# Two matmuls in place of three per 128 rows of weights in the feed-forward layers of 256 tokens

## The reference, cut to what matters

```python
def conv_ffn(h, w_up, conv_w, conv_b, w_down):
    u = h @ w_up                       # 1024 -> 2 * 2816 features
    ...
    for j in range(CONV_W):            # CONV_W = 3 taps over the tokens
        acc = acc + up[:, j:j + L] * conv_w[j]
    a, g = jnp.split(acc, 2, axis=-1)
    return (jax.nn.silu(g) * a) @ w_down
```

## Time and profile before

| | us |
|---|---|
| median of 3 runs | 1633.01 |
| lowest and highest run | 1632.73 and 1633.6 |
| span of the profiled execution | 1629.6 |
| TensorE busy in it | 1587.4 |
| VectorE busy | 1047.1 |
| ScalarE busy | 809.9 |

### The profile page before, as it was taken

The page is one execution under the profiler, slowest core; times in us unless marked ns, Lnnn a source line. Parts: engine busy times, 40 slices in busy tenths (PEclk is TensorE's granted clock), DMA queues, the critical chain, the costliest instruction groups (busy, mean ns, idle before and its releaser), DMA issues.

```text
span 1629.6 us, 27020 instructions
## 1 busy us (share of the span) xinstructions
PE 1587.4 (97%) x10876; PEld 1372.2 (84%) x10876; DVE 1047.1 (64%) x1952; ACT 809.9 (50%) x1537; POOL 236.8 (15%) x282
## 2 busy tenths in 40 slices
PE   7999999999999999999999999999999999999998
PEld 4788778877777888887899988878999898799986
DVE  3734856465345434787787767766777667767765
ACT  2414963432233323567455554655555566555553
POOL 0202320011010100012011101142111013311110
PEclk9999999999999999999999999999999999999999
DMA  9765022354564323021455453334555543345552
GB/s 365 290 247 208 24 77 103 155 207 155 207 232 181 103 97 136 27 79 53 164 185 212 169 201 124 131 105 155 182 181 182 197 140 123 133 146 187 182 194 78
DMA packets 39852, 257.29 MB, mean 158 GB/s; under 512 B 5552, under 2 KB 6832, under 8 KB 11056
## 3 DMA queue, kind: packets, MB, share of 16 engines
...
## 4 chain that ended last, share of the span: by engine, by line
PE 85%; DVE 9%; ACT 4%; issue 1%; DMA 1%; ACTq 0%; POOL 0%; DVEq 0%; SPq 0%
PE ps L486 25%; PE ps L488 25%; PE ps L487 25%; PE ps L502 3%; PE ps L634 1%; PE ps L656 1%; PE ps L643 1%; DVE ps L2101 1%; PE ps L1109 1%; DVE wl L1848 1%; PE ps L528 1%; DMA raw<-in_ada 1%; PE ps L615 1%; ACT wh L1374 1%; ACT arena L1445 1%
## 5 line engine op out<-in xcount | busy, mean ns | idle before, releaser
L1842 DVE TENSOR_TENSOR wl<-raw,wh 128x1024 fp32r<-128x1024 f32 (+3 forms) x318 | 371.1, 1208 | 346.1 <-ACT wh L1374 345.5
L1374 ACT CAST wh<-raw 128x1024 fp32r<-128x1024 f32 (+2 forms) x328 | 322.7, 1033 | 489.0 <-PE ps L488 399.2
L486 PE MATMUL ps<-xh,wh 128*128 128x256 f32 (+1 forms) x1582 | 493.6, 312 | 3.7 <-DVE wl L1848 3.2
L488 PE MATMUL ps<-xh,wl 128*128 128x256 f32 (+1 forms) x1582 | 488.6, 309 | 0.0
L487 PE MATMUL ps<-xl,wh 128*128 128x256 f32 (+1 forms) x1582 | 488.5, 309 | 0.0
L486 PEld LDWEIGHTS ps<-xh,wh 128*128 128x128 f32 x1582 | 301.8, 191 | 28.9 <-issue 9.3
L487 PEld LDWEIGHTS ps<-xl,wh 128*128 128x128 f32 x1582 | 302.0, 191 | 15.1 <-issue 0.7
L488 PEld LDWEIGHTS ps<-xh,wl 128*128 128x128 f32 x1582 | 301.9, 191 | 15.2
L486 PE MATMUL ps<-wh,xh 128*128 128x512 f32 (+3 forms) x812 | 298.6, 368 | 2.0 <-issue 0.8
L488 PE MATMUL ps<-wh,xl 128*128 128x512 f32 (+3 forms) x812 | 293.2, 361 | 0.0
L487 PE MATMUL ps<-wl,xh 128*128 128x512 f32 (+3 forms) x812 | 293.1, 361 | 0.0
...
## 6 DMA issues: line engine op xcount, KB each, us to landing
...
```

The costliest lines, as they stand in the source:

```text
L486: e.matmul(out, A[0], B[0], start=first, stop=False)
L488: return e.matmul(out, A[1], B[0], start=False, stop=last)
L1374: e.copy(hi_of(j)[:, a:b], raw_of(j)[:, a:b]).then_inc(*S.hi.up((j, half)))
L1842: e.tensor_tensor(lo_of(j)[:, a:b], raw_of(j)[:, a:b], hi_of(j)[:, a:b].bitcast(F), ALU.subtract).then_inc(*S.lo.up((j, half)))
```

## The change

The two tensors of the token side become one, `xx`, with the high and the low part as its second dimension; `xh` and `xl` are views of it. In the networks of 256 tokens the matmuls "high weights by high tokens" and "high weights by low tokens" become one of 512 columns, whose streaming operand is two runs of 256 columns: the high tokens go to columns 0 to 255 of the bank, the low ones to 256 to 511. "Low weights by high tokens" stays a matmul of 256 columns and adds to the second half (`hidden_beside`). In the last of the 8 steps the two stand the other way round.

The bank now holds the result in two halves that must be added. ScalarE copies the second half into columns 256 to 511 of the temp place; VectorE adds the first half to it there (signal `whole`, which also frees the bank). The three taps now read that sum in SBUF. On ScalarE the SiLU of chunk f - 1 stands ahead of the taps of chunk f. The network of 512 tokens is as it was.

```diff
--- before.py
+++ after.py
@@ -147,8 +147,8 @@
         return ctx.enter_context(nc.sbuf_tensor(name, shape, dt))
 
     X = sb("X", [128, 4, 1024])
-    xh = sb("xh", [128, 8, 512], R)
-    xl = sb("xl", [128, 8, 512], R)
+    xx = sb("xx", [128, 2, 8, 512], R)
+    xh, xl = xx[:, 0, :, :], xx[:, 1, :, :]
     raw = sb("raw", [128, NRAW, CH])
     wh = sb("wh", [128, NSPL, CH], R)
     wl = sb("wl", [128, NSPL, CH], R)
@@ -718,9 +718,23 @@
                 m = mm3(ps[b][:, tk], (hv[:, k, fs], lv[:, k, fs]), (xh[:, k, tk], xl[:, k, tk]), k == 0, k == 7)
             return m
 
+        def hidden_beside(up, f, part, ks=range(8)):
+
+            j, b = J[up, f], 2 * (f % 3) + part
+            hv, lv = (v.rearrange("p (k n) -> p k n", k=8) for v in (hi_of(j), lo_of(j)))
+            fs = slice(128 * part, 128 * part + 128)
+            both = ps[b][:, :].rearrange("p (s n) -> p s n", s=2)
+            for k in ks:
+                if k < 7:
+                    e.matmul(both, hv[:, k, fs], xx[:, :, k, 0:256], start=k == 0, stop=False)
+                m = e.matmul(both[:, 1, :], lv[:, k, fs], xh[:, k, 0:256], start=False, stop=False)
+                if k == 7:
+                    m = e.matmul(both, hv[:, k, fs], xx[:, :, k, 0:256], start=False, stop=True)
+            return m
+
         def hidden_free(up, f):
             for part in range(2):
-                free[2 * (f % 3) + part] = [(S.conv, (up, f, part))]
+                free[2 * (f % 3) + part] = [(S.conv, (up, f, part)) if up == "up0" else (S.vec, ("whole", up, f, part))]
 
         def by_features(up, key, g):
 
@@ -731,7 +745,7 @@
             for k in range(8):
                 wait_feature(key, k)
                 for part in range(2):
-                    m = hidden(up, 0, part, g, 256, [k])
+                    m = hidden(up, 0, part, g, 256, [k]) if up == "up0" else hidden_beside(up, 0, part, [k])
             return m
 
         def ffn(up, down, first, ngrp, ada_every=False, side=None):
@@ -752,7 +766,8 @@
                             m.then_inc(*S.proj.up(("read", up, k)))
                 for part in range(2) if ngrp == 1 or f < NT - 1 else ():
                     wait_bank(2 * (f % 3) + part)
-                    hidden(up, f, part, 0, 256 * ngrp).then_inc(*S.proj.up((up, f, part), ("use", J[up, f])))
+                    m = hidden(up, f, part, 0, 512) if ngrp == 2 else hidden_beside(up, f, part)
+                    m.then_inc(*S.proj.up((up, f, part), ("use", J[up, f])))
                 hidden_free(up, f)
                 if f >= 18 - ngrp and side:
                     next(side, None)
@@ -1545,16 +1560,29 @@
                 if f == NT - 1 and ngrp == 2:
                     split_act(0)
                 weights(after(J[up, f]))
+                for part in range(2) if ngrp == 1 else ():
+                    q.wait_ge(*S.proj.at((up, f, part)))
+                    for signal, at in wait(f):
+                        q.wait_ge(*signal.at(at))
+                    e.copy(temp(up, f)[:, part, 256:512], ps[2 * (f % 3) + part][:, 256:512]).then_inc(
+                        *S.act.up(("rest", up, f, part)))
+                if f and ngrp == 1:
+                    gate(f - 1)
                 for part in range(2):
                     w = [conv(i, f + NT * part) for i in range(4)]
-                    q.wait_ge(*S.proj.at((up, f, part)))
                     if f >= 2:
                         q.wait_ge(*S.prod.at((up, f - 2)))
-                    for signal, at in wait(f):
-                        q.wait_ge(*signal.at(at))
-                    e.activation(temp(up, f)[:, part, 0:n], ps[2 * (f % 3) + part][:, 0:n], ACT.Identity,
+                    if ngrp == 1:
+                        q.wait_ge(*S.vec.at(("whole", up, f, part)))
+                        src = temp(up, f)[:, part, 256:512]
+                    else:
+                        q.wait_ge(*S.proj.at((up, f, part)))
+                        for signal, at in wait(f):
+                            q.wait_ge(*signal.at(at))
+                        src = ps[2 * (f % 3) + part][:, :]
+                    e.activation(temp(up, f)[:, part, 0:n], src, ACT.Identity,
                                  bias=w[3], scale=w[1 if up[0] == "u" else 2]).then_inc(*S.act.up(("tap", up, f, part)))
-                if f:
+                if f and ngrp == 2:
                     gate(f - 1)
                 if f >= 18 - ngrp and side:
                     next(side, None)
@@ -2177,9 +2205,17 @@
                 if f == NT - 1 and ngrp == 2:
                     split_act(0)
                 weights(after(J[up, f]))
+                for part in range(2) if ngrp == 1 else ():
+                    rest = temp(up, f)[:, part, 256:512]
+                    q.wait_ge(*S.act.at(("rest", up, f, part)))
+                    e.tensor_tensor(rest, ps[2 * (f % 3) + part][:, 0:256], rest, ALU.add).then_inc(
+                        *S.vec.up(("whole", up, f, part)))
+                    if part:
+                        q.wait_ge(*S.vec.last())
                 for part in range(2):
                     acc = temp(up, f)[:, part, 0:n].rearrange("p (g t) -> p g t", g=ngrp)
-                    src = ps[2 * (f % 3) + part][:, 0:n].rearrange("p (g t) -> p g t", g=ngrp)
+                    src = ps[2 * (f % 3) + part][:, 0:n] if ngrp == 2 else temp(up, f)[:, part, 256:512]
+                    src = src.rearrange("p (g t) -> p g t", g=ngrp)
                     q.wait_ge(*S.act.at(("tap", up, f, part)))
                     for shift, row in others:
                         lo, hi = max(0, -shift), 256 - max(0, shift)
```

## The result

The changed kernel takes **1642.26 us** (median of 4 runs, 1640.3 to 1643.33) against 1633.3 us (4 runs, 1632.73 to 1633.67) of the kernel before beside it: a ratio of 1.0054, with a 95% interval from 1.004 to 1.0068. It is 9 us slower. The forecast was 1621.0 us, 12 us faster. Its profiled execution is the fastest of the four (1640.3 us) and has a span of 1638.8 us.

A forecast was written before the change was run, and what follows sets the result against it. TensorE, busy 97% of the span, was taken as the bound: -14.1 + 1.6 + 0.45 = -12.0 us gave a span of 1617.6, plus 3.4 for the median: 1621.0 us. Range 1618.5 to 1627.5 at 0.80.

The forecast's parts named there:

- The saved matmul (-14.1 us): TensorE in the three networks of 256 tokens: one matmul fewer in each of 1056 steps, 13.3 ns each, 14.1 us less.
- columns and 13.3 ns: TensorE's price: each matmul with its own weight load pays its columns at 2.4 GHz and a fixed 13.3 ns.
- The rival named the second run: TensorE's operand in two runs costs up to 13.3 ns more: 1626.9 us at half (chance 0.05), 1633.5 at full (0.09).
- VectorE's addition (+0.85 us per chunk): VectorE's loop: first add, middle tap and hand-overs add 1.08 us, taps from SBUF save 0.23; net +0.85.
- 57 ns: VectorE's four taps: each 0.057 us cheaper from SBUF than PSUM, 0.23 in all; bounds 0 and 0.23.
- the 0.035: Hand-over time in us, read between VectorE's taps and taken for every hand-over, including those with ScalarE.
- the idle 0.39 us in `fin0`: VectorE's idle time left per chunk of `fin0` and `fin1`: 1.45 - 0.21 - 0.85 = 0.39 us, so it keeps pace.
- That the SiLU moved ahead costs nothing: ScalarE's order: SiLU ahead of the taps costs nothing, as its input was finished 2 us before.
- GpSimd's multiply ... has most of the chunk idle: GpSimd: its multiply comes a little later per chunk, with room to spare (16 of 120 us busy).
- `up1` (+1.6 us): VectorE falls 3.6 us behind in `up1`; less 2.0 us of cushion, TensorE stands for 1.6 us.
- The ways out (+0.45 us): End of each network: the chain before the third split moves back, TensorE waits some 0.15 us, three times: 0.45 us.
- The rival that ended slower: VectorE becomes the bound: adds and middle taps run one after the other, addition 1.93 us, 1664 us; chance 0.06.

## Why the prediction was wrong, step by step

- **The saved matmul (-14.1 us): right in kind, mis-sized.** It measured -7.8 by the starts and -8.6 by the run with this part alone. The rule "columns and 13.3 ns" came from rows in which each matmul follows one of its own width. The rows of before that show a change of width were given to 0.01 us, which is not fine enough for a term of 6 ns in 350. The rival named the second run as the cause. Its size (half) came out by luck, since one run in place of two changed nothing.
- **VectorE's addition (+0.85 us per chunk): 1.26.** Taps from SBUF cost 484 ns and from PSUM 482. I had carried 57 ns over from instructions of 512 columns with other lines and operands, and kept 0 only as the other bound. The hand-overs between two engines are about 0.1 us; the 0.035 was a distance between instructions of one engine. Of the idle 0.39 us in `fin0`, 0.07 were left.
- **"That the SiLU moved ahead costs nothing": the step that failed, and with it "GpSimd's multiply ... has most of the chunk idle".** I looked only at whether the SiLU's input was ready. The step also moves whatever the SiLU releases, and GpSimd's multiply came to lie beside VectorE's low weights. That cost 0.54 us in each of eight chunks of `up1`, where VectorE was already late, 4.3 us in all. With the multiply made small 9 us came back in the whole kernel, and the time was that of before: this term, put at nothing, is what turned "no gain" into "slower". "Most of the chunk idle" spoke of GpSimd's time and not of what it disturbs. Nor would the old place have been free. The taps now read SBUF, which I had booked as a gain of 0.23 us, and with the SiLU behind them the multiply stretched the taps: 16 us more.
- **`up1` (+1.6 us): 11.** 8.6 us were lost and 2.6 us of the gain used up. Of this the borders of chunks are 7.9 us. The wait of the gates' matmul (2.4 us) was not in the sum at all: the new wait for the adds holds up ScalarE, and so the copy queued behind the middle taps. What TensorE waits for at the borders is what I had forecast, VectorE's low weights, but for about five times as long.
- **The ways out (+0.45 us): 4.1,** that is 0.7 (counted in `up1` too), 1.3 and 2.1, and behind the last one the clock of 0.51, which cost 1.6 us.
- **The rival that ended slower** had the right engine, another price (addition 1.45 and more) and another reason. VectorE became the bound in `up1` with an addition of 1.26 and the collision of 0.54.

The miss of 21 us is then made up of three parts of unlike size: about 6 us that the saved matmul didn't bring (14.1 - 7.8), about 9 us that the small multiply gives back, and about 6 us by VectorE's longer addition without the collision. The last part can be read in the run with the small multiply: TensorE stands for 3.6 us between chunks of `up1`, 2.4 at the gates and 2.3 at the ways out, 8.3 us where the forecast had 2.05. With the first and the last part alone there would have been no gain. With the second the kernel is slower.

Why `up1` loses so much more than `fin0` under the same change follows from the earlier trace rows: it had 0.72 us to spare, `fin0` 1.45. The collision also takes place in `fin0`, mostly at GpSimd's cost (its multiply takes 1.63 us in the chunk shown), but there the loop of 5.57 us just fits.

What stays open: the 2.5 ns of a pair that the order of widths doesn't explain, how much of the gain at the ways out with the small multiply is the collision and how much the shorter multiply, and why the clock fell behind some stands and not behind others.
